# A two-layer-type transformer in three-pass fp32r: high and low halves moved from separate tiles into interleaved blocks of 128 columns

## The reference, cut to what matters

```python
def first_block(x, ...):
    for l in range(DEPTH):                                   # DEPTH = 2
        x = x + 0.5 * swiglu(rms_norm(x, ffn1_norm[l]), ffn1_w1[l], ffn1_w3[l], ffn1_w2[l])
        h = rms_norm(x, mix_norm[l])
        z = h @ w_in[l]                                      # 1024 x 6752
        ...                                                  # three kinds of attention on slices of z
        mixed = (gt[:, :, 0] * (y_na @ w_br_na[l])
                 + gt[:, :, 1] * (y_gla @ w_br_gla[l])
                 + gt[:, :, 2] * (y_mla @ w_br_mla[l]))
        x = x + mixed @ w_out[l]
        x = x + 0.5 * swiglu(rms_norm(x, ffn2_norm[l]), ffn2_w1[l], ffn2_w3[l], ffn2_w2[l])

def swiglu(h, w1, w3, w2):                                   # 1024 -> 2816 -> 1024
    return (jax.nn.silu(h @ w1) * (h @ w3)) @ w2
```

## Time and profile before

| | |
|---|---|
| runs shown | 1664.19, 1666.49, 1661.94 us; median 1664.19 |
| profiled execution, first to last instruction | 1662.6 us; a time of its own around that span is not shown |
| TensorE matmul busy | 1611.2 us, 97% |
| TensorE weight load busy | 1454.2 us, 87% |
| VectorE / ScalarE / GpSimd busy | 1065.9 / 825.5 / 264.3 us |
| mean granted TensorE clock | 0.993 of full speed |
| DMA | 273.97 MB, mean 165 GB/s |

### The profile page before, as it was taken

One profiled execution on the slowest core, in us unless ns is written; L12 is line 12 of the kernel. 1 busy time (PEld: TensorE's weight loads), 2 busy tenths in 40 slices (PEclk: granted clock), 3 DMA queues, 4 the chain that ended last, 5 costly groups with the idle time before them and its releaser, 6 DMA issues.

```text
span 1662.6 us, 27116 instructions
## 1 busy us (share of the span) xinstructions
PE 1611.2 (97%) x11156; PEld 1454.2 (87%) x11156; DVE 1065.9 (64%) x1269; ACT 825.5 (50%) x1123; POOL 264.3 (16%) x208
## 2 busy tenths in 40 slices
PE   7999999999999999999999999999999999999997
PEld 7999888888989998999988888999999887879885
DVE  4655557665765455555565766566555679867985
ACT  5443446653454433543454665335443556655563
POOL 0000060010000000000034000000000069306940
PEclk9999999999999999999999999999999999999999
DMA  7757555333546655555746444255565455155612
GB/s 226 224 183 232 176 179 167 121 127 102 173 157 203 200 178 177 181 187 191 231 158 195 127 145 128 102 178 169 186 200 178 135 185 194 33 157 165 218 33 89
DMA packets 206612, 273.97 MB, mean 165 GB/s; under 512 B 18774, under 2 KB 167096, under 8 KB 206008
## 3 DMA queue, kind: packets, MB, share of 16 engines
q1 hardware_dynamic: 206376, 272.67, 51.2%
q10 hardware_dynamic: 144, 0.00, 0.0%
HBM read 271.61 MB, written 1.08 MB: 164 GB/s over the span
## 4 chain that ended last, share of the span: by engine, by line
PE 83%; DVE 11%; ACT 2%; issue 2%; POOL 1%; DMA 0%; SPq 0%; POOLq 0%; ACTq 0%; DVEq 0%
PE bank L503 29%; PE bank L550 14%; PE bank L985 8%; PE bank L974 7%; PE bank L1175 4%; DVE wlo L435 2%; PE bank L2037 2%; PE bank L2286 2%; PE bank L1257 2%; PE bank L2015 1%; PE bank L1118 1%; PE bank L956 1%; PE bank L1093 1%; ACT whi L424 1%; PE bank L2122 1%
## 5 line engine op out<-in xcount | busy, mean ns | idle before, releaser
L435 DVE TENSOR_TENSOR wlo<-raw,whi 128x2048 fp32r<-128x2048 f32 (+1 forms) x258 | 584.0, 2268 | 335.6 <-ACT whi L424 335.0
L424 ACT ACTIVATE whi<-raw 128x2048 fp32r<-128x2048 f32 (+1 forms) x258 | 484.1, 1880 | 319.6 <-PE bank L550 101.4
L503 PE MATMUL bank<-hT_hi,whi 128*128 128x256 f32 x1408 | 395.7, 281 | 0.8 <-DVE hT_lo L354 0.3
L503 PE MATMUL bank<-hT_lo,whi 128*128 128x256 f32 x1408 | 394.2, 280 | 0.0
L503 PE MATMUL bank<-hT_hi,wlo 128*128 128x256 f32 x1408 | 394.1, 280 | 0.0
L503 PEld LDWEIGHTS bank<-hT_hi,whi 128*128 128x128 f32 x1408 | 266.3, 189 | 3.5 <-issue 0.9
L503 PEld LDWEIGHTS bank<-hT_lo,whi 128*128 128x128 f32 x1408 | 266.4, 189 | 1.4
L503 PEld LDWEIGHTS bank<-hT_hi,wlo 128*128 128x128 f32 x1408 | 266.3, 189 | 0.0
L550 PE MATMUL bank<-whi,Y 128*128 128x512 f32 x704 | 223.9, 390 | 0.0
L308 POOL TENSOR_TENSOR st<-st 128x1 f32<-128x1 f32 x18 | 17.6, 980 | 938.8 <-ACT X L301 938.8
L550 PEld LDWEIGHTS bank<-whi,Y 128*128 128x128 f32 x704 | 132.2, 188 | 26.8
(11 more groups left out here) (396 smaller groups left out, 2822.6 us busy)
## 6 DMA issues: line engine op xcount, KB each, us to landing
raw<-in_ffn_w SPq DMA_DIRECT2D x132, 1024.0 KB, 5.5
raw<-in_w_in SPq DMA_DIRECT2D x80, 1024.0 KB, 5.5
raw<-in_w_out SPq DMA_DIRECT2D x16, 1024.0 KB, 4.9
raw<-in_w_br_na SPq DMA_DIRECT2D x4, 1024.0 KB, 6.0
raw<-in_w_br_mla SPq DMA_DIRECT2D x4, 1024.0 KB, 5.1
raw<-in_w_br_gla SPq DMA_DIRECT2D x4, 1024.0 KB, 5.0
raw<-in_cmp_k_w SPq DMA_DIRECT2D x4, 1024.0 KB, 6.4
raw<-in_cmp_v_w SPq DMA_DIRECT2D x4, 1024.0 KB, 5.2
```

Of the source, the lines that this page charges most:

```text
L424: act.activation(m["whi"][:, slot, 0:w], m["raw"][:, slot, 0:w], ACT.Copy).then_inc(s.hi_ready, 1)
L435: dve.tensor_tensor(m["wlo"][:, slot, 0:w], m["raw"][:, slot, 0:w], m["whi"][:, slot, 0:w].bitcast(F32), ALU.subtract).then_inc(s.lo_ready, 1)
L503: mm = pe.matmul(B[bank][:, mt * T:(mt + 1) * T], a, b, start=(n == 0 and k == 0), stop=(n == KK - 1 and k == 2))
```

## The change

The same instructions of TensorE work on the same numbers, in other places. `wsplit` takes the place of whi and wlo: for each block of 128 weight columns its high half (512 bytes) and behind it its low half. `hsplit` takes the place of hT_hi and hT_lo, and Y is laid out in the same manner, but in the other order: for each block of 128 tokens first the low half, then the high half. `halves` returns (high, low) of a token operand. A moving operand of 256 or 512 columns is now 2 or 4 runs of 128 columns, each 1,024 bytes behind the one before; a stationary operand is one run of 128 as before. ScalarE and VectorE write such runs (`blocked` gives their source the same shape). wsplit starts where whi did and Y where it did; hsplit follows Y at 114816 bytes (hsplit is as long as the two hT tiles were), so that all three start at the same place in 1,024 bytes.

Beside this, the two narrow units ("small", "sm") lie in raw at a pitch of 128 columns in place of 96 or 28, with the same elements moved; the blocks of the compressed attention are split with two instructions in place of four on ScalarE and on VectorE; and fox_r and fox_l lie in one run of Y.

```diff
+def halves(tile, k, t=None, n=1):
+    if t is not None:
+        return tile[:, NT * k + t, 1, :], tile[:, NT * k + t, 0, :]
+    return tile[:, NT * k:NT * (k + n), 1, :], tile[:, NT * k:NT * (k + n), 0, :]
+
+def blocked(a):
+    return a.rearrange("p (b n) -> p b n", n=P)
...
-        whi = sb("whi", [P, RING, UNIT], F32R)
-        wlo = sb("wlo", [P, RING, UNIT], F32R)
-        Y = sb("Y", [P, 12, 2, T], F32R)
+        wsplit = sb("wsplit", [P, RING, UNIT // P, 2, P], F32R)
+        Y = sb("Y", [P, 12 * NT, 2, P], F32R)
+        hsplit = sb("hsplit", [P, KK * NT, 2, P], F32R)
...
-        hT_hi = sb("hT_hi", [P, KK, T], F32R)
-        hT_lo = sb("hT_lo", [P, KK, T], F32R)
...
-        act.activation(m["whi"][:, slot, 0:w], m["raw"][:, slot, 0:w], ACT.Copy).then_inc(s.hi_ready, 1)
+        act.activation(self.part(slot, w, 0), self.source(slot, w), ACT.Copy).then_inc(s.hi_ready, 1)
...
-        dve.tensor_tensor(m["wlo"][:, slot, 0:w], m["raw"][:, slot, 0:w],
-                          m["whi"][:, slot, 0:w].bitcast(F32), ALU.subtract).then_inc(s.lo_ready, 1)
+        dve.tensor_tensor(self.part(slot, w, 1), self.source(slot, w), self.part(slot, w, 0).bitcast(F32),
+                          ALU.subtract).then_inc(s.lo_ready, 1)
+
+    def source(self, slot, w):
+        return blocked(self.m["raw"][:, slot, :])[:, 0:w[0], 0:w[1]]
+
+    def part(self, slot, w, part):
+        return self.m["wsplit"][:, slot, 0:w[0], part, 0:w[1]]
 
     def w(self, slot, a, n):
-        return self.m["whi"][:, slot, a:a + n], self.m["wlo"][:, slot, a:a + n]
+        b, c = a // P, a % P
+        if c + n <= P:
+            return [self.m["wsplit"][:, slot, b, part, c:c + n] for part in range(2)]
+        return [self.m["wsplit"][:, slot, b:b + n // P, part, :] for part in range(2)]
...
-        self.hid = lambda p, part: m["Y"][:, 2 * p:2 * p + 2, part, :]
+        self.hid = lambda p, part: halves(m["Y"], 2 * p, n=2)[part]
...
-                for k, (a, b) in enumerate(passes(ring.w(slot, kk * 96, 96), hT(kk))):
+                for k, (a, b) in enumerate(passes(ring.w(slot, kk * P, 96), hT(kk))):
...
             act.wait_ge(s.blk_ready, past.blk_ready + v + 1)
-            for q in range(2):
-                dst = Y[:, 8 + 2 * v + q, 0, :].rearrange("p (j g n) -> p j g n", j=8, g=2)
-                for g in range(2):
-                    ins = act.activation(dst[:, :, g, 0:N_CMP], blk[:, v, 8 * q:8 * q + 8, g, 0:N_CMP], ACT.Copy)
+            for g in range(2):
+                ins = act.activation(blk_parts(v, g)[0], blk_whole(v, g), ACT.Copy)
```

More of the change, by code:

```diff
@@ L156, in C @@
             return consts[:, a:b]
[L158 removed]
+        hT = lambda kk, t=None: halves(hsplit, kk, t)
         s = Signals(nc, ctx, SIGNALS)
@@ L546, in down_piece @@
         for mt in range(2):
-            h = [self.hid(par, part)[:, mt, t * P:(t + 1) * P] for part in range(2)]
+            h = halves(self.m["Y"], 2 * par + mt, t)
             w = self.ring.w(slot, mt * D + half * 512, 512)
@@ L771, in mix_units @@
         at += n
-        width += [{"small": 768, "uq": 1536}.get(step[0], UNIT)] * n
+        width += [{"small": (KK, 96), "uq": (12, P)}.get(step[0], WHOLE)] * n
         dmas += [2 if step[0] == "small" else 1] * n
@@ L954, in first_proj @@
             w = ring.w(slot, kk % 4 * 512, 512)
-            for k, (a, b) in enumerate(passes(hT(kk, t * P, P), w)):
+            for k, (a, b) in enumerate(passes(hT(kk, t), w)):
                 mm = pe.matmul(B[PROJ_BANK[0] + t][:, :], a, b, start=(n % KK == 0 and k == 0), stop=(n % KK == 7 and k == 2))
@@ L1172, in half_branch @@
                     w = ring.w(slot, kk * 512 + (2 * half + m2) * P, P)
-                    yk = (Y[:, y0 + kk, 0, :], Y[:, y0 + kk, 1, :])
-                    for k, (a, b) in enumerate(passes(w, yk)):
+                    for k, (a, b) in enumerate(passes(w, halves(Y, y0 + kk))):
                         mm = pe.matmul(bank[:, m2 * T:(m2 + 1) * T], a, b,
@@ L1255, in w_out @@
                 w = ring.w(slot, k2 * D + half * 512, 512)
-                for k, (a, b) in enumerate(passes(mx(2 * h + k2, t * P, P), w)):
+                for k, (a, b) in enumerate(passes(mx(2 * h + k2, t), w)):
                     mm = pe.matmul(B[2 + 2 * t + half][:, :], a, b, start=(h == 0 and k2 == 0 and k == 0),
@@ L1919, in second_layer @@
     blk = X[:, 9216:10240].rearrange("p (v j g n) -> p v j g n", v=2, j=16, g=2)
-    blk_s = lambda v, part, j: Y[:, 8 + 2 * v + j // 8, part, (j % 8) * 32:(j % 8) * 32 + 32]
+    blk_s = lambda v, j: [p[:, (j % 4) * 32:(j % 4) * 32 + 32] for p in halves(Y, 8 + 2 * v + j // 8, j // 4 % 2)]
+    blk_parts = lambda v, g: [p.rearrange("p b (j g n) -> p b j g n", j=4, g=2)[:, :, :, g, 0:N_CMP]
+                              for p in halves(Y, 8 + 2 * v, n=2)]
+    blk_whole = lambda v, g: blk[:, v, :, g, 0:N_CMP].rearrange("p (b j) n -> p b j n", b=4)
     ffT = [X[0:4, 256 * k:256 * k + T] for k in range(3)]
@@ L2044, in sm @@
             for kk in range(KK):
-                for k, (a, b) in enumerate(passes(ring.w(slot, kk * 28, 28), hT(kk))):
+                for k, (a, b) in enumerate(passes(ring.w(slot, kk * P, 28), hT(kk))):
                     mm = pe.matmul(B[3][0:28, 0:T], a, b, start=(kk == 0 and k == 0), stop=(kk == KK - 1 and k == 2))
@@ L2061, in fox_v @@
             norm.pe_wait(pe, n0, t, kk)
-            for k, (a, b) in enumerate(passes(hT(kk, t * P, P), ring.w(slot, kk * 256, 256))):
+            for k, (a, b) in enumerate(passes(hT(kk, t), ring.w(slot, kk * 256, 256))):
                 mm = pe.matmul(B[7][:, t * T:(t + 1) * T], a, b, start=(n % KK == 0 and k == 0), stop=(n % KK == 7 and k == 2))
@@ L2187, in w1 @@
                 j = 8 * (i % 2) + j8
-                left = (blk_s(v, 0, j), blk_s(v, 1, j))
-                for k, (a, b) in enumerate(passes(left, ring.w(slot, j8 * 256, 256))):
+                for k, (a, b) in enumerate(passes(blk_s(v, j), ring.w(slot, j8 * 256, 256))):
                     mm = pe.matmul(B[6][0:32, v * T:(v + 1) * T], a, b, start=(j == 0 and k == 0), stop=(j == 15 and k == 2))
@@ L2264, in pw @@
                 for kk in range(2):
-                    right = (Y[:, 2 + kk, 0, :], Y[:, 2 + kk, 1, :])
-                    for k, (a, b) in enumerate(passes(ring.w(slot, kk * 256 + mt * P, P), right)):
+                    for k, (a, b) in enumerate(passes(ring.w(slot, kk * 256 + mt * P, P), halves(Y, 2 + kk))):
                         mm = pe.matmul(B[6][:, mt * T:(mt + 1) * T], a, b, start=(kk == 0 and k == 0),
@@ L2283, in w_out @@
             for k2 in range(2):
-                left = [Y[:, 2 * h + k2, part, t * P:(t + 1) * P] for part in range(2)]
-                for k, (a, b) in enumerate(passes(left, ring.w(slot, k2 * D + half * 512, 512))):
+                for k, (a, b) in enumerate(passes(halves(Y, 2 * h + k2, t), ring.w(slot, k2 * D + half * 512, 512))):
                     mm = pe.matmul(B[OUT_BANK[2 * t + half]][:, :], a, b, start=(first and k2 == 0 and k == 0),
```

96 lines of the change are left out of this document (48 added, 48 removed).

## The result

The changed kernel takes 1678.47 us (1677.08 to 1680.1, 4 runs) against 1664.55 (1661.94 to 1666.49, 4 runs): a ratio of 1.0084, 95% interval 1.0072 to 1.0095. It is 0.8% slower, where 2.5% faster was forecast. The profiled execution's span is 1675.9 us, 13.3 longer, and its own time 1677.76.

A forecast was written before the change was run, and what follows sets the result against it. TensorE was taken as the bound, through its cost per matmul in a stream. Gains of 22.0 (feed-forwards), 18.9 (elsewhere) and 0.7 us (block splits) sum to 41.6 off, giving 1622.6 us, 2.5% less; range 1575 to 1682.

The forecast's parts named there:

- What bounds the kernel: Whole kernel: TensorE is the bound, busy 97% of the span and 83% of the chain, with much slack beside it.
- The reading of the six distances: Six matmul streams: start-to-start distances differ by operand place, 116.7 or 119.9 ns and 227.5 or 233.3, 6.7 to 20.0 over columns.
- that two streams disturb each other by the half of 512 bytes that they are in: Three-pass products: load and stream now use opposite halves of 1,024 bytes, so the excess falls to 6.7 ns.
- L2190's 113.3 ns: Stream with 32 stationary columns: constant 113.3 ns, named as the warning that a half has no meaning to the reads.
- 22.0 and 18.9 us off: Gains: 22.0 us from 44 feed-forward pairs at 0.50 each; 18.9 us elsewhere, 0.7 of 27.0.
- The price taken from L2190: Excess of 6.7 ns over the columns for every changed matmul: 113.3 ns for 256 columns, 220.0 for 512.
- Rival B: Only the small offset matters: 256 columns 119.9 ns, 512 columns 227.5, so slower at 1679 us; chance 0.23.
- Rival A: The excess nearly vanishes, all but 2.5 ns, in feed-forwards and elsewhere: 1587 us; chance 0.25.
- Rival C: Nothing changes: the excess is each stream's own price of starting an operand; 1661 to 1667 us; chance 0.14.
- The parts costed at nothing: ScalarE's and VectorE's splits writing runs of 128, and loads into raw at another pitch: each taken as 0.
- The joined block splits: Block splits: joining two of 120 saves about 0.18 us, 8 times on each engine; 0.7 us taken.
- The rules: Skill rules set against the forecast: independent read ports imply no change, 1664 us; N/2.4 + 2.5 ns implies about 1587.

The follow-up runs named there:

- the tables: Kernels that stream only float32r matmuls, 24 of each kind, other engines idle, at varied operand places; 256 columns settle at 113.3 to 120.1 ns in the sweep.
- M+0: Notation in the stream-only kernels: the moving columns' place at offset 0 bytes; with the 128 stationary columns also at 0, 256 columns take 120.0 ns.
- the sweep: Stream-only kernel, 111 kinds: moving operand's place in 32-byte steps over 1,024, then load widths and column counts; 113.3 to 120.1 ns for 256 columns.
- e3: Changed kernel with tokens laid out high|low like the weights, so load and stream always share a half: 1679.16 us, ratio 1.0076 to before.
- the first table: Stream-only kernel, 69 kinds of 24 matmuls at varied operand places; load in the same or other half: 2.87 and 2.88 us for 24.
- S+64: Kind in the stream-only kernels with the 128 stationary columns moved by 64 bytes, moving ones at 0: 113.3 ns for 256 columns.
- e1: Kernel before with x allocated behind hT_hi and hT_lo, so hT starts at the weights' place in 1,024 bytes: 1678.55 us, ratio 1.0082.
- e2: Changed kernel with hsplit allocated behind x, keeping the 32-byte offset and the blocks: 1665.41 us, ratio 1.0002 to the kernel before.
- e4: Kernel before with x behind hT and a pad, so hT starts 192 bytes off the weights within 256: 1664.84 us, ratio 0.9996.
- e7: Kernel before with a pad ahead of Y and x behind hT, so Y and hT both start 192 bytes off the weights: 1651.14 us, ratio 0.9913.
- S+8: Kind in the first table with the stationary columns moved by 8 bytes: 115.5 ns.

## Why the prediction was wrong, point by point

**What bounds the kernel: right.** TensorE's distance from start to start is the whole matter. The span grew by 13.3 us and TensorE's busy time by 13.9 (1611.2 to 1625.1), so its idle time did not grow; L435's successor shows 323.3 us of idle time before it against 323.7.

**The reading of the six distances: half right.** That equal matmuls differ by the places of their operands was right and is now shown with all other engines idle. With both operands at one place the tables have the same 13.3 ns over the columns for 256, 384 and 512 (120.0, 173.3, 226.6), as it read. That part of the excess is "a cost of the stationary load beside the moving stream" is not shown: at M+0 the sweep's loads of 48 to 112 columns give 113.3 where one of 128 gives 120, but with 512 columns a load of 64 costs more (230.6) than one of 128 (226.6). The step that failed is the next one, **that two streams disturb each other by the half of 512 bytes that they are in**. Nothing in the trace showed it. It was read off the diff, from where the operands go, and one row spoke against it: L2190's 113.3 ns, the same whichever half its load was in the earlier trace rows. The prediction named that row as the warning and then gave its mechanism 0.60 all the same. The table (2.87 and 2.88 us) and e3 put the effect of the half at zero. So the two terms of the sum that rest on it, 22.0 and 18.9 us off, do not exist: a stretch of 96 up products was to fall from 11.20 to 10.88 us and rose to 11.51, and L974's kind was to fall from 233.3 to 220 ns and fell to 226.7. What the runs showed in its place is the difference of the two operands' places within 256 bytes, which the allocation changed by 32.

**The price taken from L2190: a number that exists, in the wrong place.** 113.3 ns is the least at which 256 columns settle here. It comes with most narrower loads (the very kind of L2190 took 113.3 in the sweep and 117.8 in the first table) or with a difference of 64 or 192, in one of their rhythms, and not with the other half.

**Rival B: right, with its price.** Its sum was 1664.2 + 13.6 + 1.5 - 0.7 = 1679; measured 1678.5. A pair costs 16.98 against 16.66, 0.32 us, 14.1 us for 44 where it had 13.6. Its two small terms (1.5 and 0.7) are below what these runs resolve. It stated that Y against w "is what every pair becomes", which is what the profile shows. Its 0.23 was too low: it used only rows that existed.

**Rival A was not to be had with 256 columns.** In these float32r streams a load of 128 columns alone sets 111.6 to 111.7 ns (32 or 224 moving columns), so 109 ns a matmul lay below the load's own floor. The float32 transposes that gave the 109 have loads of 128 columns too, so their pace does not carry over.

**Rival C is out.** An excess that is each stream's own would not care about the other operand; S+64 alone takes 256 columns from 120.0 to 113.3 ns, and both moved by 32 stay at 120.0.

**The parts costed at nothing: right.** The splits (2314 against 2310 ns), the raw layout and fox's place did not show: e1, which has none of them, takes 1678.55 us and the changed kernel 1678.47. The joined block splits were 0.7 us of the sum; neither this pair nor e2, at 1.0002, can resolve that.

**The rules.** The Trainium skill, "SBUF — State Buffer", section "Who interferes with whom", has two independent read ports of TensorE. What the prediction drew from it, no effect of place, is not what the runs show: with both operands moved by 32 bytes 256 columns take 120.0 ns, with one moved 116.7 to 118.3. The Trainium skill's "TensorE: Matmul & The Clock Gate", section "Back-to-back issue gap", gives N/2.4 + 2.5 ns, 109.2 for 256, as the gap of an isolated matmul. No float32r stream of 256 columns here, with a load for each matmul, settled below 113.3.

## What to carry to other kernels

A change of layout has two parts: the layout, and where the allocation thereby puts everything behind it; undo each with one line before believing either. Where a stream of matmuls each with its own load shows two distances for one shape, sweep the difference of the two places in a kernel that does nothing else, and then sweep it again in the real order of the matmuls, since the best place of an isolated stream gave almost nothing here (1664.84) until the stream before it was moved too (1651.14). A row that stands against the mechanism one is about to price should cost it most of its chance.

## What the runs showed of the hardware that was not expected

- The distance from start to start of float32r matmuls with a stationary load each depends on the difference of the two operands' places modulo 256 bytes (in steps of 32): 113.3 to 120.1 ns for 256 columns, 226.6 to 234.1 for 512, but only 173.3 to 174.8 for 384. The best difference for 256 columns (192) is one of the worst for 512 (233.3 against 226.6 at 0). Where tokens and weights exchange their roles the difference changes its sign, which is why one offset (192 for tokens) can serve both: 113.3 and 228.9.
- A stream has more than one rhythm at the same places, and what ran before has a part in which one it takes: 10.89 and 11.31 us for the same 96 matmuls in e4, and in e7 as well. What makes it so inside the chip was not found; a conflict of reads in banks is one idea, which nothing here tests.
- Loads of 128 columns in float32r streams settle no closer than 111.6 ns at the 2.4 GHz level. The granted clock fell to its half in the sweep from 402 to 415 us, after 24 matmuls with 32 moving columns and 14 with 64; there 24 loads with 128 moving columns took 5.17 us, 213 ns each when settled.
- The runs leave open whether steps finer than 32 bytes give a better pair; the first table has hints, 115.5 ns with S+8 and 118.4 with both moved by 16.
